# Issuing the attention scores of one unit at a time instead of two, in a fused two-block kernel

## What is computed

```
score = where(allowed, score, -inf)           # index scores of 8 index heads, summed
top_s, top_i = top_k(score, 128)
s = einsum('bqgrd,bqkgd->bqgrk', q_blk, k[top_i]) * 64**-0.5
p = softmax(where(valid, s, -inf));  o = einsum('bqgrk,bqkgd->bqgrd', p, v[top_i])
```

## Time and profile before

| | |
|---|---|
| median of 3 runs | 2002.42 us (2002.15 to 2004.39) |
| the profiled execution | 2002.15 us, span 2000.4 us |
| PE busy | 1935.1 us, 97% of the span |
| DVE busy, ACT busy | 1245.1 us (62%), 862.1 us (43%) |
| mean granted PE clock | 0.986; 1.00 from 1412 us to 1565 us |
| units of the sparse attention | from 1412.3 us to 1564.5 us of the span |

### The profile page before, as it was taken

How to read it: one execution, slowest core, us unless ns; L and a number is a source line. 1 busy time by engine, 2 the same in 40 slices (tenths; PEclk the granted TensorE clock), 3 DMA queues, 4 the chain that set the end, 5 groups by cost and what they waited for, 6 DMA issues and landing times.

```text
span 2000.4 us, 23124 instructions
## 1 busy us (share of the span) xinstructions
PE 1935.1 (97%) x8436; PEld 1509.7 (75%) x8436; DVE 1245.1 (62%) x1864; ACT 862.1 (43%) x1175; POOL 0.2 (0%) x4
## 2 busy tenths in 40 slices
PE   6999899899999999999999999998999999999999
PEld 4888587677777777788888876665766788888887
DVE  5999879767575748644443365588666565444322
ACT  5444555344444435544432234455344444444221
POOL 0000000000000000000000000000000000000000
PEclk8999899999999999999999999998999999999999
DMA  4332243221211112323233322111221233233333
GB/s 174 103 96 89 81 132 117 81 78 47 69 56 58 56 53 95 98 92 105 94 95 121 121 87 82 53 42 53 74 74 42 95 95 109 90 105 94 105 96 105
DMA packets 49281, 175.70 MB, mean 88 GB/s; under 512 B 6064, under 2 KB 6192, under 8 KB 48432
## 3 DMA queue, kind: packets, MB, share of 16 engines
q1 hardware_dynamic: 44640, 160.19, 25.2%
q10 hardware_dynamic: 4560, 14.41, 2.1%
HBM read 166.71 MB, written 6.29 MB: 86 GB/s over the span
## 4 chain that ended last, share of the span: by engine, by line
PE 80%; DVE 14%; ACT 4%; issue 2%; ACTq 0%; DMA 0%; DVEq 0%
PE ps L1570 66%; PE ps L1586 2%; PE ps L1770 2%; DVE w_lo L953 2%; PE ps L1621 2%; PE ps L1772 1%; PE ps L1798 1%; PE ps L1789 1%; ACT w_hi L435 1%; DVE cv_acc L1132 1%; DVE ds_acc L1327 1%; PE ps L1945 1%; DVE X L1005 1%; PE ps L1996 1%; DVE ds_mx L1326 1%
## 5 line engine op out<-in xcount | busy, mean ns | idle before, releaser
L953 DVE TENSOR_TENSOR w_lo<-w_raw,w_hi 128x1024 fp32r<-128x1024 f32 x299 | 365.7, 1224 | 367.8 <-ACT w_hi L435 361.7
L1570 PE MATMUL ps<-H_hi,w_hi 128*128 128x512 f32 x1272 | 509.0, 400 | 1.0 <-DVE H_lo L999 1.0
L1570 PE MATMUL ps<-H_hi,w_lo 128*128 128x512 f32 x1272 | 495.7, 390 | 0.0
L1570 PE MATMUL ps<-H_lo,w_hi 128*128 128x512 f32 x1272 | 495.5, 390 | 0.0
L435 ACT ACTIVATE w_hi<-w_raw 128x1024 fp32r<-128x1024 f32 x299 | 313.7, 1050 | 245.8 <-PE ps L1570 170.5
L1570 PEld LDWEIGHTS ps<-H_hi,w_hi 128*128 128x128 f32 x1272 | 239.2, 188 | 58.0 <-issue 7.4
L1570 PEld LDWEIGHTS ps<-H_lo,w_hi 128*128 128x128 f32 x1272 | 239.2, 188 | 55.3 <-issue 6.7
L1570 PEld LDWEIGHTS ps<-H_hi,w_lo 128*128 128x128 f32 x1272 | 239.0, 188 | 50.5
L1570 PE MATMUL ps<-mid_hi,w_lo 128*128 128x512 f32 x352 | 138.7, 394 | 0.0
L1570 PE MATMUL ps<-mid_hi,w_hi 128*128 128x512 f32 x352 | 138.7, 394 | 0.0
L1570 PE MATMUL ps<-mid_lo,w_hi 128*128 128x512 f32 x352 | 138.7, 394 | 0.0
(11 more groups left out here) (337 smaller groups left out, 2685.9 us busy)
## 6 DMA issues: line engine op xcount, KB each, us to landing
w_raw<-weights SPq DMA_DIRECT2D x299, 512.0 KB, 3.5
X<-x ACTq DMA_DIRECT2D x4, 512.0 KB, 11.2
pl_P<-spill ACTq DMA_DIRECT2D x1, 2048.0 KB, 7.9
spill<-X ACTq DMA_DIRECT2D x8, 256.0 KB, 2.0
X<-spill ACTq DMA_DIRECT2D x2, 1024.0 KB, 5.0
out<-X SPq DMA_DIRECT2D x8, 256.0 KB, 4.6
at_mask<-masks ACTq DMA_DIRECT2D x1, 1536.0 KB, 6.1
at_pair<-at_raw ACTq DMA_DIRECT2D x96, 16.0 KB
```

The source lines that it names most:

```text
L953: dve.tensor_tensor(w_lo[:, s, :], w_raw[:, s, :], w_hi[:, s, :].bitcast(F32), ALU.subtract)\
L1570: mm = pe.matmul(ps[:, bank, :], w, x, start=first and n == 0 and q == 0, stop=last and n == len(blocks) - 1 and q == 2)
```

## The change

Before, the function `two_scores` issued S(u+2) and S(u+3) together in each even step u, after one wait for M(u+1). Now `scores` issues one S(u+2) in every step u from 0 to 29, right behind T(u), after a wait for M(u). S(0) and S(1) are still issued together. No arithmetic, buffer or other engine's instruction changes.

```
-            def two_scores(first):
-                if first:
-                    pe.wait_ge(m_done, k.up(m_done, 2))
-                for u in (first, first + 1):
-                    c, half, b = SPARSE_UNITS[u]
-                    rows = slice(HEAD * half, HEAD * half + HEAD)
-                    pe.matmul(ps[:, 4 + u % 2, 0:P * (b + 1)], ds_U[rows, c, b * P:(b + 1) * P],
-                              ds_kvi[rows, 0, 0:P * (b + 1)], start=True, stop=True).then_inc(s_done, 1)
-                    k.up(s_done)
+            def scores(u):
+                c, half, b = SPARSE_UNITS[u]
+                rows = slice(HEAD * half, HEAD * half + HEAD)
+                if u >= 2:
+                    pe.wait_ge(m_done, k.up(m_done))
+                pe.matmul(ps[:, 4 + u % 2, 0:P * (b + 1)], ds_U[rows, c, b * P:(b + 1) * P],
+                          ds_kvi[rows, 0, 0:P * (b + 1)], start=True, stop=True).then_inc(s_done, 1)
+                k.up(s_done)
...
-                    two_scores(0)
+                    scores(0)
+                    scores(1)
...
-                if u < 30 and u % 2 == 0:
-                    two_scores(u + 2)
+                if u < 30:
+                    scores(u + 2)
```

## The result

| | before | changed |
|---|---|---|
| median | 2002.54 us (5 runs, 2002.15 to 2004.39) | 2011.52 us (5 runs, 2009.0 to 2018.68) |
| profiled execution | 2002.15 us | 2012.62 us |
| its span | 2000.4 us | 2010.8 us |
| PE busy | 1935.1 us | 1948.5 us |

The changed kernel is slower: ratio 1.0052, with a 95% interval of 1.0031 to 1.0074, which is 6 to 15 us. The forecast was 2006.6 us in a range up to 2009.0, so the direction was right, and the size was less than half of what came.

What follows compares the result with a forecast made beforehand. PE sets the early pace, later a DVE loop, and delays pass on whole. Delays of 0.95-1.85, 0.72-0.82, 0.48-0.58, 1.32-1.52 and 0.1-0.3 sum to 3.6-5.1 us; 4.2 taken gives 2006.6 us, range 2003.2 to 2009.0.

Steps and rivals of the forecast that it cites:

- What bounds the kernel: PE sets the pace in steps 0 to 8, later a loop through DVE; stage 10's delay is passed on in full.
- the 0.18 us counted for it in step 20: Scores start 0.66 us after T(20) but 0.48 after T(18), so the removed wait was valued at 0.18 us.
- The two halves run at the same time, so parting costs: Even and odd scores on different 64 rows overlap; a pair costs 0.20 us more than one whole-array matmul.
- The price of a lone score, s = p + 0.05: One 64-row score costs a whole-array matmul's price p plus 0.05 us, with ends p and p + 0.1.
- rival 1: A lone score costs half of the pair and parting nothing: sum -0.3 us, 2002.1 us; chance 13%.
- The result comes p + 0.30 after the start: A score's result follows its start by the whole-array matmul's price p plus 0.30 us, taken from the index scores.
- The overrun of the idle time at T(24) and T(28), 0.1 to 0.3: Lone scores between fills use up PE's 0.69 us idle time there and overrun it by 0.1 to 0.3 us.
- Steps 10 to 16, "nothing more": DVE and ACT lead; lone scores disappear in PE's idle time at T(12), T(14) and T(16), adding no delay.
- The sum: The steps' delays add 3.6 to 5.1 us, middle 4.3; 4.2 was taken, giving 2006.6 us.
- rival 2: A lone score costs as much as the pair, p + 0.20: 6.7 us more, 2009.1 us; chance 15%.
- The prediction's own sign of being wrong, over 2.5 us at T(9): Forecast had T(9) about 1.2 us later; a distance to before already over 2.5 us there would refute it.
- The span rule of the Trainium skill: Matmuls in different row groups run at once, 4 ns per further one; read strictly, 2009.1 us.

Runs made afterwards that it cites:

- the same-half experiment: Kernel of before, order and waits kept, but both scores of a pair read partitions 0 to 63: ratio 1.0031 (1.0017 to 1.0046).
- the second build: The changed kernel built again with no edit: ratio 1.0042 (1.0027 to 1.0057) to before, T(0) to T(31) 151.25 us.

## Why the prediction was wrong

- *What bounds the kernel*: right. The delay was passed on whole, and M(20), M(23), M(27) and M(31) waited for lone scores in the places named. The removed wait was worth next to nothing (0.16 us in all), and the 0.18 us counted for it in step 20 was not its doing: with the old wait put back, S(22) still started 0.48 us after T(20), since PE came later by then.
- *The two halves run at the same time, so parting costs*: right, and shown by the same-half experiment (1.91 against 1.05 us).
- *The price of a lone score, s = p + 0.05*: **this step failed.** It is p + 0.20, the pair's. With 0.05 for the lone score, the sum left 0.15 of the pair's 0.20 to its second score. The passes show that this one costs nothing; all of it is the change from 128 rows to 64 and back. The earlier trace rows measured only the way in (0.1), and I took that row as the upper end. The pair itself was the nearest row for the same instruction in the same place, and it had been pushed out to a rival with 15%. The sentence that no row shows one unit alone was also too strong: the group at 1320.13 us is on one half alone, between whole-array matmuls, and costs 0.20 more than its four p. It excludes rival 1 and gives s = p + 0.20.
- *The result comes p + 0.30 after the start*: too short as well. M(31) started 1.27 us after S(31) (1568.23 to 1569.50) instead of 1.16, and M(20) 1.05 after S(20) instead of 0.95.
- *The overrun of the idle time at T(24) and T(28), 0.1 to 0.3*: too small. Less the delay of the last M before each, T(20), T(24) and T(28) came 0.21, 0.29 and 0.29 us late, 0.8 in all, and T(20) had no such term.
- *Steps 10 to 16, "nothing more"*: wrong by 0.22 us. M(17) started 1.05 us after S(17), as the M do that wait for a lone score of 384 columns, and passed this on to M(20).
- *The sum*: rival 2 was the case that came. It gave 2.75 us for M(11) (measured 2.91) and 6.7 for the stage (7.67). The rest is spread over all steps, 0.16 in M(11), 0.38 in M(20), 0.30 in M(23) and 0.16 in M(27) and M(31), mostly by the three terms above. The prediction's own sign of being wrong, over 2.5 us at T(9), came: it was 2.63.
- The span rule of the Trainium skill ("TensorE: Matmul & The Clock Gate", "Measured speedup vs the span model") holds here: it has a second matmul on other rows cost 4 ns, and the trace has 1.05 us for a pair and 1.05 to 1.06 for one.
- *The total*: 7.67 us on 2002.5 is 2010.2. The first median was 2011.5; the interval of its ratio allows 6 to 15 us, that of the second build 5 to 11. In the profiled execution the part beyond 7.67 us is the clock ahead of the stage; for the median it is likely the same, but not shown. Rival 1 (half the price) is excluded by the rows.

## What to carry to other kernels

In this kernel two matmuls on the two halves of the array are one job: the second one is free as long as it stands next to the first, and a wait of 0.2 us ahead of the pair is far cheaper than parting it (1.06 us at 512 columns). Where the rows at hand hold only the pair, the lone one should be priced like the pair until a row shows otherwise, and such a row is worth looking for in all stages, by the shape and the rows of the array, and not by the line. And when a few microseconds of a 2 ms program are at stake, one reads the stretch between two instructions of the changed stage, since totals move by as much with the clock in stages that were not touched.

## What was not expected of the hardware

- A whole-array fp32 matmul, with twice the rows, was cheaper alone than one on half of the array: 0.86 against 1.06 us at 512 columns ahead of O, and 0.22 against 0.61 us at 128 columns between a transpose and a fill.
- In three of the eleven traces the granted clock fell right after PE had idled 1.1 to 1.6 us at T(14) (to 0.58 in 1498 to 1502 us, between the two levels of 1.2 and 2.4 GHz), and the step from T(14) to T(15) took at least 1.5 us longer than in before. In the other eight, after idle times of 0.9 to 1.7 us there, it stayed at 1.00. What decides it stays open.
